# Second-layer weight chunks of 256 neighbouring rows, two to a partition, in a one-core mixture-of-experts encoder layer

## The chip, the cores and the metric

One core of a Trainium2 chip runs the whole layer. The metric is the device time of one execution in microseconds. The kernel before takes 1170.18 us, the median of 3 runs (1169.88 to 1171.66).

## What is computed

The layer takes 256 tokens of width 1024, all in float32. First comes the token mixer: RMSNorm, a combined projection, four heads of gated linear attention and eight heads of ordinary attention, and an output projection with a residual. Then comes the mixture of experts, in which most of the time lies:

```
logits = xt @ w_router + b_router              # 32 experts, each token goes to its best 4
gates  = softmax(top 4 logits)
per expert e, for the rows routed to it:
    h      = xb @ w1[e] + b1[e]                # 1024 -> 2048
    h_glu  = min(h[:, :1024], 7)
    h_lin  = clip(h[:, 1024:], -7, 7)
    act    = h_glu * sigmoid(1.702 * h_glu) * (h_lin + 1)      # the SwiGLU tile
    y      = act @ w2[e] + b2[e]               # 1024 -> 1024
out = h + sum over the 4 experts of gate * y, then a last RMSNorm
```

The weights of one expert are 8 MB of `w1[e]` and 4 MB of `w2[e]`, and those of all 32 experts are read from HBM once.

## The kernel before

**Stages.** The engines' programs are written out by hand, one after the other, and talk by semaphores. About the first 165 us are the token mixer, the router and its tables. Then `expert(n, q, it)` (L1303 to L1352 on TensorE, L931 to L950 on VectorE, L558 to L572 on ScalarE) runs once for each expert, in rounds of 64 tokens (`CAP`) per expert. The first four experts are written out, and the other 28 are a loop of bodies of four.

**Weights.** A ring of 16 slots, each 8 KB in every partition, holds chunks of weights. An expert has 12 chunks: 8 of the first layer (128 rows of `w1[e]`, each 8 KB, one to a partition, L316) and 4 of the second (L319). Each is one DMA of 1024 KB, all issued by SyncE in the order of use. SyncE waits at `refill` (L350 to L358) until TensorE has used the chunk that had the slot (`chunk_used`), and then issues the next one, 16 chunks ahead. Four more chunks lie in the scratch area `work` in the beginning (`load_early`).

**One expert on TensorE.** The hidden layer is kept as a tile of 128 partitions by 512 columns: partition `j * 64 + c` is token slot c with half j of the hidden columns (`GROUPS` is 2, `FG` is 512). (1) L1238 puts the bias into banks 2 and 5. (2) The first layer, L1319: 8 chunks of 4 matmuls each; between them four `combine` matmuls (L1288) add the expert before to the output. (3) `gather(n + 1)` (L1281): 48 short bf16 matmuls fetch the tokens of the next expert. (4) L1332: four transposes of `lin`, the SwiGLU tile, which VectorE has ready after L943, L944, L946 and L949. (5) L1341: two transposes of the gates. (6) ScalarE copies the four transposes out of bank 5 into `hidT` (L563). (7) The second layer, L1349: 4 chunks of 4 matmuls, with `hidT` as the stationary operand and the weights streaming. ScalarE copies the result out (L571), and VectorE's L943 of the next expert starts when its first layer is done.

**The rows of a second-layer chunk.** In the kernel before, chunk s holds, in partition p, rows `s * 128 + p` and `512 + s * 128 + p` of `w2[e]`: two separate runs of 4 KB (`by_half`, L278). Transposed block s of `lin` has the hidden columns `s * 128 + p` of both halves side by side, so that one block serves one chunk.

In the built program the operand that a transpose loads as its weights is `lin`, and the identity matrix streams.

Of the kernel before, what the change touches and what calls it, by code (L numbers as in the profile page):

```python
# [27 lines left out]
P = 128  # L28
SEQ = 256
TILES = SEQ // P  # L30
D = 1024
# [24 lines left out]
CAP = 64  # L56
GROUPS = P // CAP
ROUNDS = SEQ // CAP
FG = FF // GROUPS
SUB = FG // P  # L60
# [7 lines left out]
PEELED = EARLY_AT + EARLY + SLOTS  # L68
W1_CHUNKS = KD
W2_CHUNKS = SUB  # L70
PER_EXPERT = W1_CHUNKS + W2_CHUNKS
UNROLL = 4
PER_BODY = UNROLL * PER_EXPERT
assert PER_BODY % SLOTS == 0 and EXPERTS % UNROLL == 0 and GROUPS * 1024 == SLOT
LOADS_PER_BODY = PER_BODY // SLOTS
assert all(c % PER_EXPERT for c in range(EARLY_AT, EARLY_AT + EARLY))
TABLE = ROUNDS * EXPERTS + UNROLL
# [26 lines left out]
def encoder_layer(nc, x, w_in, w_out, w_router, w1, b1, w2, b2, gate_w, columns, rows, final_g,  # L104
                  c_keep, c_front, later, split, out):
    ctx = ExitStack()
    with ctx:
# [11 lines left out]
        ident, iota, before, ones = (ckeep[:, i * P:(i + 1) * P] for i in range(4))  # L119
# [104 lines left out]
        lin = back(FG)  # L224
        sig = back(FG)
        hidT = back(SUB, P)
# [12 lines left out]
        bank = [ctx.enter_context(nc.psum_tensor(f"bank{i}", [P, 512], F32))[:, :] for i in range(8)]  # L239
# [26 lines left out]
        def slot_of(c):  # L266

            return (c - EARLY) % SLOTS

        def first_slot_of(c):  # L270

            return c % SLOTS

        def slot(s):
            return ring[:, s * SLOT:(s + 1) * SLOT]

        def by_half(chunk):

            return chunk.rearrange("p (j n) -> p j n", n=D)


        @block.sync
        def _(sp):
# [16 lines left out]
            def load_b1(n, e):  # L300
                sp.dma_start(b1_sb[n % 2].rearrange("j (g f) -> j g f", g=2),
                             b1[e].rearrange("(g j f) -> j g f", g=2, j=GROUPS)).then_inc(b1_in[n % 2], 16)
# [10 lines left out]
            def load(to, loaded, e, r):  # L313

                if r < W1_CHUNKS:
                    sp.dma_start(to, w1[e, r * P:(r + 1) * P, :]).then_inc(loaded, 16)  # L316
                else:
                    s = r - W1_CHUNKS
                    sp.dma_start(by_half(to), w2[e].rearrange("(j s p) n -> s p j n", j=GROUPS, p=P)[s]).then_inc(loaded, 16)  # L319

            def first_ring(s):
                load(slot(s), slot_in[s], s // PER_EXPERT, s % PER_EXPERT)

            def load_early(i):
                load(early[i], early_in[i], (EARLY_AT + i) // PER_EXPERT, (EARLY_AT + i) % PER_EXPERT)

# [22 lines left out]
            def refill(it, used, e):  # L349

                c = SLOTS + used
                q, r = divmod(c, PER_EXPERT)
                if r == 0:
                    sp.wait_ge(S.chunk_used, it * PER_BODY + ((q - 2) * PER_EXPERT + W1_CHUNKS))
                    load_b1(q, e)
                sp.wait_ge(S.chunk_used, it * PER_BODY + (used + 1))
                load(slot(slot_of(c)), slot_in[slot_of(c)], e, r)
# [15 lines left out]
            start = PEELED - SLOTS  # L373
# [5 lines left out]
            last = rounds * bodies + whole  # L379
# [616 lines left out]
        def _(pe):  # L996
            mm = nc.tensor.matmul
# [4 lines left out]
            for pair in range(KD // 2):  # L1002
                if pair >= 2:
                    pe.wait_ge(S.xT_v if pair == 2 else S.xT_a, 2)
                for k in (2 * pair, 2 * pair + 1):
                    for t in range(TILES):
                        o = (k % 2) * SEQ + t * P
                        last = nc.tensor.transpose(bank[6 + pair % 2][:, o:o + P], h[:, t, k * P:(k + 1) * P], ident)
                last.then_inc(S.xT_ps, 1)

            def xT(k, t=None):
                return turned[:, k, :] if t is None else turned[:, k, t * P:(t + 1) * P]


            for k in range(KD):
# [4 lines left out]
                def put(o, l, r, first):  # L1020
                    return mm(o, l, r, start=a and first, stop=z, skip_group_check=True)  # L1021
# [6 lines left out]
                for t in range(TILES):  # L1028
                    put(bank[3 + t][:, :], xT(k, t), w[:, C_AQ:C_AK], True)
                    last = put(bank[5][:, t * SEQ:(t + 1) * SEQ], xT(k, t), w[:, C_AK:D_IN], t == 0)  # L1030
# [20 lines left out]
            for k in range(KD):  # L1051
                for t in range(TILES):
                    last = mm(bank[6 + t][:, :], xT(k, t), w_in_sb[:, k, C_GV:C_GR], start=k == 0, stop=k == KD - 1)
# [16 lines left out]
            for k in range(KD):  # L1070
                for t in range(TILES):
                    last = mm(bank[3 + t][:, :], xT(k, t), w_in_sb[:, k, C_GR:C_ZG], start=k == 0, stop=k == KD - 1)
# [129 lines left out]
            def router(t):  # L1202
                for k in range(KD):
                    if k % 4 == 0:
                        pe.wait_ge((S.hT_v, S.hT_a)[k // 4], t + 1)
                    last = mm(bank[6][:, t * EXPERTS:(t + 1) * EXPERTS], xT(k, t), wr_sb[:, k, :], start=k == 0, stop=k == KD - 1)
                return last
# [4 lines left out]
            for t in range(TILES):  # L1212
                if t == 1:
                    pe.wait_ge(S.ogla_sb, TILES)
                for k in range(4):
                    for nb in range(2):
                        last = mm(bank[Y[2 * t + nb]][:, :], xT(4 + k, t), w_out_att[:, k, nb * 512:(nb + 1) * 512],  # L1217
                                  start=k == 0, stop=False, skip_group_check=True)
# [4 lines left out]
            for t in range(TILES):  # L1223
                pe.wait_ge((S.glaT_v, S.glaT_a)[t], 1)
                for k in range(4):
                    if t == 1 and k == 2:
                        turn_h(0)
                    for nb in range(2):
                        last = mm(bank[Y[2 * t + nb]][:, :], xT(k, t), w_out_gla[:, k, nb * 512:(nb + 1) * 512],  # L1229
                                  start=False, stop=k == 3, skip_group_check=True)  # L1230
# [5 lines left out]
            def start_hidden(g, q):  # L1236

                mm(bank[(2, 5)[g]][:, :], split_of(q % 2), b1_sb[q % 2][:, g * FG:(g + 1) * FG], start=True, stop=False,  # L1238
                   skip_group_check=True)
# [7 lines left out]
            last = router(1)  # L1247
# [45 lines left out]
            def loaded(q, r, it):  # L1293

                c = q * PER_EXPERT + r
                first = isinstance(it, int)
                if first and c < EARLY_AT:
                    pe.wait_ge(slot_in[first_slot_of(c)], (c // SLOTS + 1) * 16)
                    return slot(first_slot_of(c))
                if first and c < EARLY_AT + EARLY:  # L1300
                    pe.wait_ge(early_in[c - EARLY_AT], 16)
                    return early[c - EARLY_AT]
                pe.wait_ge(slot_in[slot_of(c)], (it * LOADS_PER_BODY + ((c - EARLY) // SLOTS + 1)) * 16)  # L1303
                return slot(slot_of(c))

            def expert(n, q, it, first=False, second=False):


                if not first:
                    pe.wait_ge(b1_in[q % 2], (it * (UNROLL // 2) + (q // 2 + 1)) * 16)  # L1310
                    start_hidden(1, q)
                    pe.wait_ge(S.res_ready, n)
                    start_hidden(0, q)
                pe.wait_ge(S.xg_ready, n + 1)
                for k in range(W1_CHUNKS):
                    chunk = loaded(q, k, it)
                    for j in range(GROUPS):
                        for g in range(2):
                            last = mm(bank[(2, 5)[g]][j * CAP:(j + 1) * CAP, :], xg[:, k * CAP:(k + 1) * CAP],  # L1319
                                      chunk[:, g * FF + j * FG:g * FF + (j + 1) * FG], start=False, stop=k == KD - 1,  # L1320
                                      skip_group_check=True)
                    last.then_inc(S.chunk_used, 1)

                    if second and k % 2 == 0:
                        start_row(k // 2)
                    if not first and k % 2 == 1:
                        combine(k // 2)
                gather(n + 1)

                pe.wait_ge(S.hid_ready, n + 1)  # L1330
                for s in range(SUB):
                    last = nc.tensor.transpose(bank[5][:, s * P:(s + 1) * P], lin[:, s * P:(s + 1) * P], ident)  # L1332
                last.then_inc(S.hidT_ps, 1)

                pe.wait_ge(S.gated_ready, n + 1)
                if first:
                    pe.wait_ge(S.gateT_sb, 1)
                else:
                    pe.wait_ge(S.gatedT_sb, n)
                for t in range(TILES):  # L1340
                    last = nc.tensor.transpose(bank[7][:, t * P:(t + 1) * P], gated[:, t, :], ident)  # L1341
                last.then_inc(S.gatedT_ps, 1)
                pe.wait_ge(S.hidT_sb, n + 1)

                for s in range(W2_CHUNKS):
                    chunk = by_half(loaded(q, W1_CHUNKS + s, it))
                    for half in range(GROUPS):
                        for j in range(GROUPS):
                            last = mm(bank[2][j * CAP:(j + 1) * CAP, :], hidT[:, s, half * CAP:(half + 1) * CAP],  # L1349
                                      chunk[:, half, j * 512:(j + 1) * 512], start=s == 0 and half == 0,  # L1350
                                      stop=s == SUB - 1 and half == GROUPS - 1, skip_group_check=True)
                    last.then_inc(S.chunk_used, 1)  # L1352

            for t in range(TILES):
# [17 lines left out]
            for nb in range(2):  # L1372
                last = mm(bank[5 + nb][:, :], ones[FIN_G_ROW:FIN_G_ROW + 1, :], fin_g[:, nb * 512:(nb + 1) * 512],
                          start=True, stop=True)
# [48 lines left out]
```

## Time and profile before

| | |
|---|---|
| Median of 3 runs | 1170.18 us (1169.88 to 1171.66) |
| Span of the profiled execution | 1170.7 us |
| The profiled execution's own time outside its span | not given apart |
| TensorE matmul busy | 1113.7 us, 95% |
| VectorE, ScalarE, GpSimd busy | 212.8, 117.3, 18.9 us |
| DMA packets' time, share of 16 engines' span | 89.7% |
| Mean granted TensorE clock | 0.984 of full speed |

A matmul in float32 stands in the profile as two MATMUL records with a LDWEIGHTS record each. "PE" is TensorE's matmul side, "PEld" its weight loads, "SPq" SyncE's queue. "Idle before" is the time that an engine stood still before an instruction, with what released it. A busy TensorE says little by itself; what matters is which wait ends last in each stage.

### The profile page before, as it was taken

Reading aid. Unit: us, or ns where it says so; the run is one execution under the profiler, and the core shown is the slowest. Engines: PE = TensorE matmul, PEld = TensorE weight load, DVE = VectorE, ACT = ScalarE, POOL = GpSimd, SP = SyncE. Lnnn points to the kernel's source line nnn. Section 1 sums busy time; section 2 is a strip of 40 time slices with the busy share of each in tenths; the row PEclk is TensorE's granted clock in tenths of the full one; section 3 lists DMA queues with packets and bytes.
Section 4 is the critical chain, followed back from the end, with each engine's and each line's share of the span. In section 5 each row is a group of like instructions: output and inputs, shape, how many; then the busy total and the mean of one; then the engine's idle time right before and its main releaser. Section 6 shows DMA issues by size and latency. Waiting matters only on the chain.

```text
span 1170.7 us, 14556 instructions
## 1 busy us (share of the span) xinstructions
PE 1113.7 (95%) x5873; PEld 440.4 (38%) x5873; DVE 212.8 (18%) x491; ACT 117.3 (10%) x226; POOL 18.9 (2%) x18
## 2 busy tenths in 40 slices
PE   7997989999999999999999999999999999999996
PEld 4645443333333333333333333333333333333332
DVE  1186251111111110111111111111111111011113
ACT  1053120000000000000000000000000000000002
POOL 0010020000000000000000000000000000000000
PEclk9997979999999999999999999999999999999998
DMA  9655529988999999999999999999999999999940
GB/s 372 176 204 225 218 113 405 345 358 324 407 411 404 408 406 412 405 410 405 413 400 408 408 405 408 406 404 411 413 406 413 408 405 404 413 410 406 405 169 36
DMA packets 75952, 420.28 MB, mean 359 GB/s; under 512 B 6869, under 2 KB 7129, under 8 KB 42138
## 3 DMA queue, kind: packets, MB, share of 16 engines
q1 hardware_dynamic: 75930, 419.98, 89.7%
q8 instruction: 15, 0.25, 0.1%
q14 instruction: 7, 0.06, 0.0%
HBM read 418.91 MB, written 1.05 MB: 359 GB/s over the span
## 4 chain that ended last, share of the span: by engine, by line
PE 83%; DVE 10%; ACT 3%; issue 3%; DMA 0%; POOL 0%; SPq 0%; POOLq 0%; DVEq 0%
PE bank L1319 40%; PE bank L1349 20%; PE bank L1288 9%; PE bank L1238 5%; PE bank L1021 4%; DVE work L949 2%; DVE work L946 2%; DVE work L944 2%; PE bank L1332 2%; ACT work L563 2%; PE bank L1229 1%; PE bank L1217 1%; DMA h<-in_x_dram 0%; ACT work L513 0%; DVE work L943 0%
## 5 line engine op out<-in xcount | busy, mean ns | idle before, releaser
L1319 PE MATMUL bank<-ring,work 128*64 128x512 f32 x2016 | 468.0, 602 | 0.4 <-DVE work L928 0.4
L1319 PEld LDWEIGHTS bank<-ring,work 128*64 128x64 f32 x2016 | 154.2, 136 | 298.2 <-issue 297.3
L1349 PE MATMUL bank<-ring,work 128*64 128x512 f32 x1024 | 228.5, 599 | 15.5 <-ACT work L563 15.5
L943 DVE TENSOR_SCALAR work<-bank 128x512 f32<-128x512 f32 x32 | 22.1, 692 | 829.0 <-PE bank L1319 829.0
L1288 PE MATMUL bank<-work 64*128 64x512 f32 x256 | 141.2, 640 | 0.7 <-ACT work L571 0.7
L1349 PEld LDWEIGHTS bank<-ring,work 128*64 128x64 f32 x1024 | 71.7, 137 | 151.7 <-issue 134.0
L560 ACT ACTIVATE work<-work 128x512 f32<-128x512 f32 x32 | 20.2, 630 | 639.2 <-DVE work L943 639.2
L1288 PEld LDWEIGHTS bank<-work 64*128 64x128 f32 x256 | 37.2, 184 | 102.7 <-issue 101.1
L1238 PE MATMUL bank<-biases,split_sb 2*128 2x512 f32 x128 | 64.5, 622 | 0.0
L1281 PE MATMUL bank<-work,tok 128*128 128x64 bf16 x1056 | 50.8, 194 | 0.0
L1281 PE MATMUL bank<-work 128*128 128x64 bf16 x528 | 48.9, 195 | 1.2 <-DVE work L921 1.2
L1281 PEld LDWEIGHTS bank<-work,tok 128*128 128x128 bf16 x1056 | 47.4, 99 | 0.0
L1281 PEld LDWEIGHTS bank<-work 128*128 128x128 bf16 x528 | 33.5, 99 | 25.6 <-issue 25.6
L571 ACT ACTIVATE work<-bank 128x512 f32<-128x512 f32 x32 | 19.1, 597 | 223.4 <-PE bank L1349 223.4
L1238 PEld LDWEIGHTS bank<-biases,split_sb 2*128 2x128 f32 x128 | 21.2, 185 | 40.7 <-issue 25.3
L1332 PE MATMUL bank<-ckeep,work 128*128 128x128 f32 x128 | 21.0, 286 | 9.9 <-DVE work L949 9.9
L397 POOL TENSOR_TENSOR stat<-stat 128x1 f32<-128x1 f32 (+2 forms) x8 | 9.1, 1136 | 1105.2 <-DVE stat L604 1105.2
L563 ACT ACTIVATE work<-bank 128x512 f32<-128x512 f32 x32 | 19.1, 597 | 68.3 <-PE bank L1332 68.3
L928 DVE TENSOR_TENSOR work<-bank,col 128x512 f32<-128x512 f32 x33 | 22.6, 684 | 0.8 <-PE bank L1281 0.8
L949 DVE TENSOR_TENSOR work<-work 128x512 f32<-128x512 f32 x32 | 22.1, 692 | 1.1
L946 DVE SCALAR_TENSOR_TENSOR work<-work 128x512 f32<-128x512 f32 x32 | 22.1, 692 | 1.1
L936 DVE TENSOR_SCALAR work<-ckeep,work 128x128 f32<-128x128 f32 x64 | 19.3, 344 | 15.4 <-PE bank L1341 15.4
(185 smaller groups left out, 479.2 us busy)
## 6 DMA issues: line engine op xcount, KB each, us to landing
ring<-in_w_dram SPq DMA_DIRECT2D x380, 1024.0 KB, 7.9
ring<-in_w_in_dram SPq DMA_DIRECT2D x8, 1168.0 KB, 15.9
work<-in_w_dram SPq DMA_DIRECT2D x4, 1024.0 KB, 8.2
ring<-in_w_out_dram SPq DMA_DIRECT2D x2, 1024.0 KB, 27.5
ring<-in_w_out_dram SPq DMA_DIRECT2D x1, 2048.0 KB, 29.7
h<-in_x_dram SPq DMA_DIRECT2D x2, 512.0 KB, 4.5
out_dram<-tok SPq DMA_DIRECT2D x4, 256.0 KB, 2.2
biases<-in_b_dram SPq DMA_DIRECT2D x32, 8.0 KB
```

What stands on the lines that cost most here:

```text
L563: nc.scalar.activation(hidT, bank[5][:, :].rearrange("p (s q) -> p s q", q=P), ACT.Copy)\
L928: nc.vector.tensor_tensor(xg.rearrange("p (k c) -> p k c", c=CAP), bank[6][:, :].rearrange("p (k c) -> p k c", c=CAP), ffn_g.rearrange("p ...
L944: nc.vector.tensor_scalar(lin, bank[5][:, :], LIMIT, -LIMIT, ALU.min, ALU.max).then_inc(S.dve_step, 1)
L946: nc.vector.scalar_tensor_tensor(lin, lin, 1.0, glu, ALU.add, ALU.mult).then_inc(S.dve_step, 1)
L949: nc.vector.tensor_tensor(lin, lin, sig, ALU.mult).then_inc(S.hid_ready, 1)
L1021: return mm(o, l, r, start=a and first, stop=z, skip_group_check=True)
L1238: mm(bank[(2, 5)[g]][:, :], split_of(q % 2), b1_sb[q % 2][:, g * FG:(g + 1) * FG], start=True, stop=False, skip_group_check=True)
L1281: last = mm(bank[6][:, k * CAP:(k + 1) * CAP], parts[t][i][:, k * P:(k + 1) * P], onehot[:, t, :], start=i == 0 and t == 0, stop=i == PART ...
L1288: last = mm(bank[Y[i]][:, :], gatedT[j * CAP:(j + 1) * CAP, t, :], res[j * CAP:(j + 1) * CAP, :], start=False, stop=stop, skip_group_check ...
L1319: last = mm(bank[(2, 5)[g]][j * CAP:(j + 1) * CAP, :], xg[:, k * CAP:(k + 1) * CAP], chunk[:, g * FF + j * FG:g * FF + (j + 1) * FG], star ...
L1332: last = nc.tensor.transpose(bank[5][:, s * P:(s + 1) * P], lin[:, s * P:(s + 1) * P], ident)
L1349: last = mm(bank[2][j * CAP:(j + 1) * CAP, :], hidT[:, s, half * CAP:(half + 1) * CAP], chunk[:, half, j * 512:(j + 1) * 512], start=s == ...
```

## The change

Second-layer chunk s now holds rows `s * 256` to `s * 256 + 255` of `w2[e]`, and partition p the rows `s * 256 + 2p` and `s * 256 + 2p + 1`, one run of 8 KB. Chunks 0 and 1 belong to half 0 of the hidden columns, chunks 2 and 3 to half 1. For the stationary operand to fit, a transposed block takes every second column of `lin`: block `b * 2 + r` has the columns `b * 256 + 2p + r`. Each transpose's weight load therefore reads 128 float32 values that lie 8 bytes apart, not 4. The number, sizes and order of all instructions on each engine are as before, and so is every wait.

```diff
+PAIR = 2
+BLOCKS = FG // (PAIR * P)
...
                 else:
                     s = r - W1_CHUNKS
-                    sp.dma_start(by_half(to), w2[e].rearrange("(j s p) n -> s p j n", j=GROUPS, p=P)[s]).then_inc(loaded, 16)
+                    sp.dma_start(to, w2[e].rearrange("(s p j) n -> s p (j n)", j=PAIR, p=P)[s]).then_inc(loaded, 16)
...
                 pe.wait_ge(S.hid_ready, n + 1)
-                for s in range(SUB):
-                    last = nc.tensor.transpose(bank[5][:, s * P:(s + 1) * P], lin[:, s * P:(s + 1) * P], ident)
+                pairs = lin.rearrange("p (b c r) -> p b c r", c=P, r=PAIR)
+                for b in range(BLOCKS):
+                    for r in range(PAIR):
+                        s = b * PAIR + r
+                        last = nc.tensor.transpose(bank[5][:, s * P:(s + 1) * P], pairs[:, b, :, r], ident)
                 last.then_inc(S.hidT_ps, 1)
...
                 for s in range(W2_CHUNKS):
-                    chunk = by_half(loaded(q, W1_CHUNKS + s, it))
-                    for half in range(GROUPS):
+                    chunk = by_row(loaded(q, W1_CHUNKS + s, it))
+                    half, b = divmod(s, BLOCKS)
+                    for r in range(PAIR):
                         for j in range(GROUPS):
-                            last = mm(bank[2][j * CAP:(j + 1) * CAP, :], hidT[:, s, half * CAP:(half + 1) * CAP],
-                                      chunk[:, half, j * 512:(j + 1) * 512], start=s == 0 and half == 0,
-                                      stop=s == SUB - 1 and half == GROUPS - 1, skip_group_check=True)
+                            last = mm(bank[2][j * CAP:(j + 1) * CAP, :], hidT[:, b * PAIR + r, half * CAP:(half + 1) * CAP],
+                                      chunk[:, r, j * 512:(j + 1) * 512], start=s == 0 and r == 0,
+                                      stop=s == SUB - 1 and r == PAIR - 1, skip_group_check=True)
                     last.then_inc(S.chunk_used, 1)
```

## Rows read from the trace of the kernel before

**Rows 1.** The page's totals: busy us (share) xinstructions, and the DMA queue with packets.

```profile
PE 1113.7 (95%) x5873; PEld 440.4 (38%) x5873; DVE 212.8 (18%) x491; ACT 117.3 (10%) x226; POOL 18.9 (2%) x18
...
DMA packets 75952, 420.28 MB, mean 359 GB/s; under 512 B 6869, under 2 KB 7129, under 8 KB 42138
...
q1 hardware_dynamic: 75930, 419.98, 89.7%
```

**Rows 2.** All waits of TensorE that the profile names: us in total, times, longest us.

```profile
PE bank L1349 <- ACT work L563: 15.5, 32, 0.5
PE bank L1332 <- DVE work L949: 9.9, 32, 1.3
PE bank L1008 <- DMA h<-in_x_dram: 7.6, 1, 7.6
```

**Rows 3.** SyncE's waits: us in total, times, longest us.

```profile
SPq L316 <- PE bank L1349: 245.4, 118, 5.4
SPq L316 <- PE bank L1319: 233.0, 116, 3.5
SPq L319 <- PE bank L1319: 227.8, 124, 10.5
```

**Rows 4.** Windows, each from L943 to the next L943; last columns: granted clock, DMA share, GB/s.

```profile
183.32:220.57 37.25, 35.45 (x169) 11.50 (x169) 4.20 (x9) 2.10 (x4) 0.00 (x0) 0.95 1.00 393
251.44:282.30 30.86, 30.12 (x163) 11.02 (x163) 4.20 (x9) 2.10 (x4) 0.00 (x0) 1.00 0.86 345
405.85:436.71 30.86, 30.12 (x163) 11.04 (x163) 4.20 (x9) 2.10 (x4) 0.00 (x0) 1.00 1.01 407
1116.25:1147.12 30.87, 30.13 (x163) 11.03 (x164) 4.20 (x10) 2.10 (x4) 0.00 (x0) 1.00 0.27 106
```

**Rows 5.** The chain of waits from 407.1 us: start us, us, what.

```profile
407.17 0.70 DVE work L946
...
407.89 0.70 DVE work L949
...
408.64 0.67 PE bank L1332 x4
...
409.33 0.60 ACT work L563
...
409.99 1.07 PE bank L1349 x3
```

**Rows 6.** Timeline of the same place: start us, us, what [idle before <-releaser].

```profile
408.64 0.42 PEld L1332 LDWEIGHTS bank<-ckeep,work 128*128 128x128 f32 x4 [0.40 <-DVE work L949]
408.64 0.65 PE L1332 MATMUL bank<-ckeep,work 128*128 128x128 f32 x4 [0.28 <-DVE work L949]
```

**Rows 7.** L1332's weight loads, ns min/median/max; then page groups, busy us, mean ns.

```profile
L1332 PEld LDWEIGHTS bank<-ckeep,work x128: 137/141/143, 186.1 to 1150.2; 128*128 128x128 f32 x128
...
L1319 PEld LDWEIGHTS bank<-ring,work 128*64 128x64 f32 x2016 | 154.2, 136 | 298.2 <-issue 297.3
...
L1288 PEld LDWEIGHTS bank<-work 64*128 64x128 f32 x256 | 37.2, 184 | 102.7 <-issue 101.1
...
L1281 PE MATMUL bank<-work,tok 128*128 128x64 bf16 x1056 | 50.8, 194 | 0.0
```

**Rows 8.** Windows inside one expert; last columns as in rows 4.

```profile
419.00:423.00 4.00, 4.00 (x17) 1.43 (x18) 0.00 (x0) 0.00 (x0) 0.00 (x0) 1.00 1.01 426
...
409.00:413.00 4.00, 3.53 (x19) 1.34 (x19) 1.12 (x5) 0.87 (x2) 0.00 (x0) 1.00 1.02 410
```

**Rows 9.** Timeline: when SyncE issues, around the same expert.

```profile
401.37 4.98 SPq L319 DMA_DIRECT2D ring<-in_w_dram  x3
...
412.10 15.70 SPq L316 DMA_DIRECT2D ring<-in_w_dram  x8
```

**Rows 10.** The page's median time from issue to landing of the ring's chunks, in us.

```profile
ring<-in_w_dram SPq DMA_DIRECT2D x380, 1024.0 KB, 7.9
```

**Rows 11.** A window in the first expert's second layer; last columns as in rows 4.

```profile
187.60:191.00 3.40, 3.40 (x10) 0.97 (x11) 0.36 (x3) 0.09 (x1) 0.00 (x0) 0.50 1.03 413
```

More of the change, by code:

```diff
@@ L275, in slot, with by_row @@
             return ring[:, s * SLOT:(s + 1) * SLOT]
-        def by_half(chunk):
-            return chunk.rearrange("p (j n) -> p j n", n=D)
+        def by_row(chunk):
+            return chunk.rearrange("p (r n) -> p r n", n=D)
         @block.sync
```

## The prediction

> **What bounds the kernel now.** I read the page's totals first, then TensorE's and SyncE's waits, then windows one expert long, and last the chain of waits inside one expert.
>
> The totals leave two candidates: TensorE is busy for 95% of the span, and the DMA engines for 89.7% [rows 1]. Neither share says which one the other waits for. The waits do. TensorE waits for a DMA once, 7.6 us at the very start for `x`, and never for a chunk of weights; in the experts its named waits are for VectorE before the transposes and for ScalarE before the second layer, 32 times each, 9.9 and 15.5 us in all [rows 2]. SyncE waits for TensorE to give chunks free, 245.4 + 233.0 + 227.8 = 706 us [rows 3]. The transfers follow TensorE, and not the other way round.
>
> The windows say it more strongly. From one L943 to the next an expert takes 30.86 us when the DMA engines are busy for a share of 0.86, 30.86 us at 1.01, and 30.87 us at 0.27, near the end, when hardly a chunk is left to fetch [rows 4]. TensorE is busy for 30.12 or 30.13 us of each. So in the experts the time is TensorE's 30.1 us plus 0.74 us of idle time, and neither the transfers' speed nor their traffic shows in it. The 32 L943 lie in 183.32 to 1147.12 us: 31 periods, of which the first is 37.25 us and the others nearly alike.
>
> The 0.74 us of idle time lies at the activation. The chain ends on VectorE with L946 and L949 (L943 and L944 stand before them), then come the four transposes L1332 (0.67 us), ScalarE's copy L563 (0.60 us), and the second layer L1349 [rows 5]. TensorE has nothing else to do between L949 and L1349 but the six transposes. So whatever is added to L1332 is added to the expert, 32 times.
>
> **The change part by part.**
>
> *The transfers of the second layer.* 128 of the 384 chunks are fetched in runs of 8 KB and no longer of 4 KB. 32 experts x 4 chunks x 256 runs = 32,768 of the 42,138 packets under 8 KB [rows 1] become 16,384 of 8 KB. What is that worth to the DMA engines? SyncE issues L319's chunks from 401.37 us and L316's from 412.10 us [rows 9], and a chunk lands a median 7.9 us after its issue [rows 10]; so the window 409 to 413 us carries second-layer chunks, and 419 to 423 us first-layer chunks, whose runs are already 8 KB. They show 410 and 426 GB/s at the same full share [rows 8]. Four chunks, 4.19 MB, would take 9.8 us at 426 GB/s and not 10.2 us: 0.4 us of DMA time less per expert. All of it lies beside TensorE's work, and I count it as 0. Its cover is TensorE's period: an expert needs 12.58 MB, or 8.39 / 426 + 4.19 / 410 = 19.7 + 10.2 = 29.9 us, against 30.86. If that cover were gone, the 0.4 us would count in full (rival 2). The change only makes the cover thicker, to 29.5.
>
> *Order and use of the chunks.* SyncE issues as many DMAs at the same points with the same waits. A chunk holds the same 8 KB per partition at the same place in its slot, and the four matmuls on it stream the same halves of 512 columns with 64 stationary columns each. Only which block of `hidT` goes with which chunk differs, and all four blocks come from one copy, L563, before the first of these matmuls. This costs 0 and moves no wait: the release of each chunk still stands after its fourth matmul.
>
> *The four transposes.* Their streaming side, the identity, is as before; so are their writes to bank 5 and the copy behind them. What changes is the weight load, which now reads every second float32 of `lin`. The trace of before has no strided weight load, so I bound it. Below, the cost is 0: reading 128 values spread over twice the bytes gives no reason to be quicker than reading them side by side. Above, each load of 141 ns [rows 7] takes twice as long with nothing of it hidden: 4 x 0.141 x 32 = 18.0 us. Between the ends, the rows say what hides a load. The four loads together are busy for 0.42 us and the four multiplications follow them at that pace, 0.105 us each, although one load lasts 141 ns: a load runs under the multiplication before it [rows 6, 7]. Only the first has none before it, because TensorE has been idle for 0.28 us. What reading more costs there: a load of 128 columns is 184 ns and one of 64 is 136 ns [rows 7], 48 ns for 64 columns. If a step of two makes 128 columns cost like 192 to 256, that is 0.048 to 0.096 us on the first load, and times 32, 1.5 to 3.1 us. I take 0, because of the gather's loads, the nearest row on how fast TensorE can read weights: 33 gathers of 48 matmuls, each with a load of 128 bf16 columns, or 256 bytes per partition, are busy for 50.8 us [rows 7], 0.032 us each or 8.0 bytes per ns. A transpose's load has 0.105 us. Its 512 bytes need 4.9 bytes per ns in that time; if the gaps count as if they were read, 1024 bytes need 9.8. The former lies well within what the gather shows, the latter a fifth above it, which is why rival 1 stays alive.
>
> A rule bears on this. The Trainium skill, "Advanced Engine Details and Errata", section SBUF Cachelines, says that SBUF has lines of 16 bytes, that at least two hits on a line are needed for full speed, and that a different line for each access costs. A step of two float32 gives exactly two hits per line, so by that rule the loads cost nothing more, on the edge of it; a step of four would pay. No row of this trace tests it.
>
> *Sum.* 0 + 0 + 0 against a profiled span of 1170.7 us, whose time outside the span isn't given; the span is 0.5 us above the median and within the spread of the 3 runs. I set the forecast against the median: **1170.2 us**.
>
> **The rivals.** What a measurement of this kernel can tell from no change is about 0.2%, 2.3 us.
>
> 1. *The strided loads become the pace of the transposes (slower).* If a load's read takes longer than the 0.105 us of the multiplication that covers it, all four are exposed. At twice the pace L1332 takes 0.42 us more in each expert, and L563 and L1349 start that much later: 0.42 x 32 = 13.4 us, 1183.6 us. For it: nothing lies between L949 and L563 but these transposes [rows 5]. Against it: if only the wanted bytes count, the gather's loads read faster than this asks for [rows 7]. It decides from 0.105 us of reading on. Its mild form, only the first load longer, gives 1.5 to 3.1 us: 1171.7 to 1173.3.
>
> 2. *The transfers bound the experts after all (faster).* Their share is 1.01 for most of the run [rows 4], and 29.9 us of transfers is only 1.0 us below the period. If they set the period, 0.4 us comes off in each of the some 27 experts at that share: 10.8 us, 1159.4 us. Against it: no wait for a chunk in [rows 2], and the same period at a share of 0.27 [rows 4]. I see almost no room for it. The Trainium skill's page "Perfetto Trace Analysis", section What "DMA-bound" means, says that large descriptors are what matters where the DMA engines bind; by it this change would pay here if the share alone were looked at.
>
> 3. *The granted clock shifts.* In the first expert's second layer TensorE runs at 0.50 (the lower level, 1.2 GHz) for 3.40 us, right behind the idle time at its activation [rows 11]. At 2.4 GHz the same work takes 1.7 us, so losing this stretch gives 1168.5 us, and one more like it 1171.9. This stays within 0.2%.
>
> 4. *The change doesn't do what it says*: the DMA still goes out in 4 KB packets. Time as before, 1170.2 us, since the transfers are hidden either way.
>
> **How the numbers follow.** No change, rivals 3 and 4 with it: 0.83, at 1170.2. Rival 1 in full: 0.08. Its mild form: 0.05, of which 0.03 stays within 0.2%. Rival 2: 0.04. So faster 0.04, same 0.83 + 0.03 = 0.86, slower 0.08 + 0.02 = 0.10. The range goes from the clock's 1168.5 to the mild form's upper end, 1173.3, and leaves out rival 2 and the full rival 1, 0.12 together.
>
> **What would show it.** Right: from L943 to the next L943 again 30.87 us; the transposes' loads at about 141 ns, and four transposes in 0.67 us; packets under 8 KB down from 42,138 to about 9,400; the window of second-layer chunks at some 426 GB/s; SyncE's waits for TensorE longer, since chunks land sooner; TensorE still with no wait for a chunk. Rival 1: the four transposes longer than 0.67 us, with L563 idle that much longer. Rival 2: a period under 30.8 us. The prediction is wrong if the transposes take over 0.07 us more per expert, or if the time before the first L943, 183.32 us, moves by over 2 us, which nothing here leads me to expect.

## The result and the profile after

The changed kernel takes 1173.41 us (median of 6 runs, 1172.38 to 1174.94), the kernel before 1170.69 us in the same comparison (6 runs, 1168.87 to 1171.66). The ratio is 1.0029 with a 95% interval of 1.0017 to 1.0040: slower by 0.3%, 2.7 us. The forecast was 1170.2 us and no change; the measured time lies just above the top of the range, 1173.3. The six times of each kernel fall in two groups of three, 1172.4 and 1174.4 to 1174.9 us for the changed kernel, 1168.9 to 1170.2 and 1171.2 to 1171.7 us for the kernel before, and each median lies between its groups.

The page's totals of the changed kernel answer to [rows 1]:

```profile
PE 1116.2 (95%) x5873; PEld 442.9 (38%) x5873; DVE 212.7 (18%) x491; ACT 117.3 (10%) x226; POOL 18.9 (2%) x18
...
DMA packets 59568, 420.28 MB, mean 358 GB/s; under 512 B 6869, under 2 KB 7129, under 8 KB 9370
...
q1 hardware_dynamic: 59546, 419.98, 88.9%
```

The 8 KB runs are there: packets under 8 KB fell from 42,138 to 9,370, and the DMA engines' share from 89.7% to 88.9%. TensorE's busy time grew by 2.5 us with the same number of instructions. Its waits are those of [rows 2], to the tenth in the experts:

```profile
PE bank L1355 <- ACT work L565: 15.5, 32, 0.5
PE bank L1337 <- DVE work L951: 9.9, 32, 1.3
PE bank L1010 <- DMA h<-in_x_dram: 7.5, 1, 7.5
```

So no wait of TensorE was added and none taken away; something that TensorE or the chain behind it does takes longer. Two windows of the changed kernel, with the columns of [rows 4]. The first is one expert, from L945 (the old L943) to the next L945; the second carries second-layer chunks and answers to the last of [rows 8]:

```profile
405.89:436.85 30.96, 30.22 (x163) 11.12 (x163) 4.20 (x9) 2.10 (x4) 0.00 (x0) 1.00 1.00 412
408.00:412.00 4.00, 3.26 (x31) 1.76 (x29) 2.16 (x6) 0.87 (x2) 0.00 (x0) 1.00 1.02 426
```

An expert takes 30.96 us instead of 30.86, and TensorE is busy for 30.22 us of it instead of 30.12. The transfers got faster, 426 GB/s instead of 410. That is one window of 4 us; the same window in the 12 experts behind it shows 420 to 424 GB/s, and 410 or 411 in the kernel before. So the gain is some 3%, and it is worth nothing. The experts behind the first all show the difference. The last L945 of the changed kernel comes 929.23 us after its second one; in the kernel before the same 30 periods take 1147.12 - 220.57 = 926.55 us [rows 4]. That is 2.68 us over 30 experts, 0.089 us each:

```profile
220.07 0.69 DVE L945 TENSOR_SCALAR work<-bank 128x512 f32<-128x512 f32 x1 [32.60 <-PE bank L1321]
...
1149.30 0.69 DVE L945 TENSOR_SCALAR work<-bank 128x512 f32<-128x512 f32 x1 [26.10 <-PE bank L1321]
```

The place of the loss shows in the chain of waits of the changed kernel, which answers to [rows 5]:

```profile
407.22 0.70 DVE work L948
...
407.94 0.70 DVE work L951
...
408.69 0.76 PE bank L1337 x4
...
409.48 0.61 ACT work L565
...
410.12 1.07 PE bank L1355 x3
```

The four transposes take 0.76 us and not 0.67; all other links have their old length to 0.01 us. The durations of these instructions in the changed kernel and in the kernel before (ns min/median/max, first and last start) say how:

```profile
L1337 PEld LDWEIGHTS bank<-ckeep,work x128: 194/209/222, 185.5 to 1152.4; 128*128 128x128 f32 x128
L1337 PE MATMUL bank<-ckeep,work x128: 281/283/387, 185.5 to 1152.6; 128*128 128x128 f32 x128
```

```profile
L1332 PE MATMUL bank<-ckeep,work x128: 272/273/330, 186.1 to 1150.3; 128*128 128x128 f32 x128
```

A load takes 209 ns instead of 141 [rows 7]. Of the four multiplications, three went from 273 to 283 ns. The maximum, which belongs to the first of a group, whose load nothing covers, went from 330 to 387. 57 + 3 x 10 = 87 ns per expert, and times 32 that is 2.8 us. The records overlap, so durations alone could mislead, but the start times say the same. As medians over the 32 experts, the four multiplications start 2, 167, 277 and 386 ns after the first load in the kernel before, and 2, 224, 344 and 464 ns after it in the changed one: 57 ns later behind the first, then some 10 ns more for each.

### The profile page after: what moved, and what is told of

Same layout as the page of the kernel before. It is cut to its first block, busy times and chain, and to the rows that moved or that the text cites. A ratio compares the mean times of both kernels' runs of the same rounds, so it can differ in the third digit from the quotient of the medians.

```text
span 1173.0 us, 14556 instructions
## 1 busy us (share of the span) xinstructions
PE 1116.2 (95%) x5873; PEld 442.9 (38%) x5873; DVE 212.7 (18%) x491; ACT 117.3 (10%) x226; POOL 18.9 (2%) x18
## 2 busy tenths in 40 slices
DMA packets 59568, 420.28 MB, mean 358 GB/s; under 512 B 6869, under 2 KB 7129, under 8 KB 9370
## 3 DMA queue, kind: packets, MB, share of 16 engines
q1 hardware_dynamic: 59546, 419.98, 88.9%
## 4 chain that ended last, share of the span: by engine, by line
PE 83%; DVE 10%; ACT 3%; issue 2%; DMA 0%; POOL 0%; SPq 0%; POOLq 0%; DVEq 0%
PE bank L1321 40%; PE bank L1355 19%; PE bank L1290 9%; PE bank L1240 5%; PE bank L1023 3%; PE bank L1337 2%; DVE work L951 2%; DVE work L948 2%; DVE work L946 2%; ACT work L565 2%; PE bank L1231 1%; PE bank L1219 1%; ACT work L515 0%; DMA h<-in_x_dram 0%; DVE work L945 0%
## 5 line engine op out<-in xcount | busy, mean ns | idle before, releaser
L1355 PE MATMUL bank<-ring,work 128*64 128x512 f32 x1024 | 228.5, 599 | 15.5 <-ACT work L565 15.5
L945 DVE TENSOR_SCALAR work<-bank 128x512 f32<-128x512 f32 x32 | 22.1, 692 | 829.0 <-PE bank L1321 829.0
L1337 PE MATMUL bank<-ckeep,work 128*128 128x128 f32 x128 | 23.8, 309 | 9.9 <-DVE work L951 9.9
L1337 PEld LDWEIGHTS bank<-ckeep,work 128*128 128x128 f32 x128 | 17.8, 208 | 13.7 <-DVE work L951 13.7
## 6 DMA issues: line engine op xcount, KB each, us to landing
ring<-in_w_in_dram SPq DMA_DIRECT2D x8, 1168.0 KB, 15.5
```

The costliest lines, as they stand in the source:

```text
L1337: last = nc.tensor.transpose(bank[5][:, s * P:(s + 1) * P], pairs[:, b, :, r], ident)
L1355: last = mm(bank[2][j * CAP:(j + 1) * CAP, :], hidT[:, b * PAIR + r, half * CAP:(half + 1) * CAP], chunk[:, r, j * 512:(j + 1) * 512], sta ...
```

## The experiments

Theory A: the weight loads with a step of two columns are the whole cost. Theory B: the 8 KB transfers disturb TensorE. Theory C: the difference comes from outside the experts. All comparisons below have the kernel before on the same chip. The first four experiments share its 26 runs (median 1170.04 us), the last four its 7 runs (1170.62 us).

**e1_runs_only.** The changed kernel with the transposes of before:

```diff
-                        last = nc.tensor.transpose(bank[5][:, s * P:(s + 1) * P], pairs[:, b, :, r], ident)
+                    last = nc.tensor.transpose(bank[5][:, s * P:(s + 1) * P], lin[:, s * P:(s + 1) * P], ident)
```

> Only the 8 KB runs are kept; the transposes read neighbouring columns again, so that a chunk's rows of w2 meet other hidden columns than they belong to (same work, other pairing). Theory A (the weight load with a step of two columns is the whole cost): four transposes back at 0.67 us, loads at 141 ns, period of an expert 30.87 us, time level with before (ratio 1.000, within 0.001). Theory B (the 8 KB transfers disturb TensorE or what feeds it): period near 30.96 us, ratio near 1.0025. Theory C (the measured 2.7 us comes from outside the experts): period 30.87 us and ratio still near 1.0025.

Measured: 1169.87 us (12 runs), ratio 0.9998 (0.9988 to 1.0007). One expert lies between these two rows of its timeline, 30.87 us:

```profile
403.10 0.69 DVE L945 TENSOR_SCALAR work<-bank 128x512 f32<-128x512 f32 x1 [26.09 <-PE bank L1321]
433.97 0.69 DVE L945 TENSOR_SCALAR work<-bank 128x512 f32<-128x512 f32 x1 [26.06 <-PE bank L1321]
```

The loads are back at 140 ns. Theories B and C fall: with the 8 KB runs alone, the time is that of before. The 30 periods behind the first expert take 926.55 us (217.82 to 1144.37), as in the kernel before to the hundredth.

**e2_step_only.** The kernel before with the changed kernel's transposes and its own 4 KB runs:

```diff
-                    last = nc.tensor.transpose(bank[5][:, s * P:(s + 1) * P], lin[:, s * P:(s + 1) * P], ident)
+                        last = nc.tensor.transpose(bank[5][:, s * P:(s + 1) * P], pairs[:, b, :, r], ident)
```

> Only the transposes' step of two columns is put into the kernel before; the chunks are fetched in 4 KB runs as before, so the pairing of rows and hidden columns is off (same work). Theory A: loads near 209 ns, period near 30.96 us, 32 x 0.09 = 2.9 us, ratio 1.0025. Theory B: period 30.87 us, ratio 1.000. Theory C: period 30.87 us.

Measured: 1174.37 us (6 runs), ratio 1.0033 (1.0021 to 1.0044). The transposes of this kernel, and one expert of 30.96 us:

```profile
L1337 PEld LDWEIGHTS bank<-ckeep,work x128: 194/209/222, 184.2 to 1149.5; 128*128 128x128 f32 x128
L1337 PE MATMUL bank<-ckeep,work x128: 281/283/387, 184.2 to 1149.6; 128*128 128x128 f32 x128
```

```profile
402.90 0.69 DVE L945 TENSOR_SCALAR work<-bank 128x512 f32<-128x512 f32 x1 [26.10 <-PE bank L1321]
433.86 0.69 DVE L945 TENSOR_SCALAR work<-bank 128x512 f32<-128x512 f32 x1 [26.06 <-PE bank L1321]
```

The same durations as in the changed kernel, with the old transfers, and 929.24 us for the 30 periods (217.08 to 1146.32) against the changed kernel's 929.23. The step of two alone makes the whole difference, and theory A stands: one half of the change costs 2.8 us and the other is worth 0.

**e5_step4.** As e2_step_only, but the values of a load lie 16 bytes apart, and the pairing is off here too:

```diff
-PAIR = 2
+PAIR = 4
```

> As the kernel before, but the transposes step by four columns (16 bytes), so the pairing of rows and hidden columns is off. If a load's cost grows with the bytes it spans (+68 ns from step one to two), loads near 345 ns, the multiplications paced by them at some 0.25 us, period 31.4 to 31.6 us, 17 to 22 us more in all. If each value then needs a line of its own and two were free, the same or worse. If any step but one costs the same: loads 209 ns, period 30.96 us, 2.9 us more.

Measured: 1173.39 us (6 runs), ratio 1.0030 (1.0019 to 1.0042).

```profile
L1337 PEld LDWEIGHTS bank<-ckeep,work x128: 195/212/222, 184.7 to 1150.0; 128*128 128x128 f32 x128
L1337 PE MATMUL bank<-ckeep,work x128: 283/285/388, 184.7 to 1150.1; 128*128 128x128 f32 x128
```

The cost does not grow with the bytes spanned: a step of four is 212 ns, a step of two 209, a step of one 141. Of the two steps tried, both pay about 70 ns. My expectation of 345 ns was wrong, and the third case written down, that any step but one costs the same, held for these two steps. The prediction drew on a rule here: by the Trainium skill, "Advanced Engine Details and Errata", section SBUF Cachelines, at least two hits on a line of 16 bytes are needed for full speed. The prediction took two hits to be enough. The trace does not bear that out for this weight load: a step of two gives two hits and pays 68 ns, and a step of four, with one hit, pays only 3 ns more. The measurement decides.

**e3_sorted.** The 8 KB runs kept, the sorting moved from TensorE's weight load to VectorE's last multiplication, and the transposes reading its new tile:

```diff
-                nc.vector.tensor_tensor(lin, lin, sig, ALU.mult).then_inc(S.hid_ready, 1)
+                by_parity = [a.rearrange("p (b c r) -> p b r c", c=P, r=PAIR) for a in (lin, sig)]
+                nc.vector.tensor_tensor(glu.rearrange("p (b r c) -> p b r c", c=P, r=PAIR), *by_parity, ALU.mult)\
+                    .then_inc(S.hid_ready, 1)
```

> The change with the sorting moved to VectorE: its last multiplication of the SwiGLU tile reads both operands with a step of two columns and writes the result side by side into another tile, and the transposes read neighbouring columns. Theory A: loads at 141 ns, period 30.87 us if VectorE reads with a step of two at its old 692 ns, ratio 1.000; if that multiplication gets longer by x ns, the period gets longer by x as well, since it stands right ahead of the transposes. Theory B: period 30.96 us or more.

Measured: 1169.93 us (11 runs), ratio 1.0001 (0.9993 to 1.0010). The multiplication and the transposes' loads of this kernel:

```profile
L952 DVE TENSOR_TENSOR work<-work x32: 691/692/693, 184.6 to 1146.6; 128x512 f32<-128x512 f32 x32
```

```profile
L1336 PEld LDWEIGHTS bank<-ckeep,work x128: 138/140/143, 185.3 to 1147.7; 128*128 128x128 f32 x128
```

VectorE reads both operands with a step of two at its old 692 ns. This version does all that the change does, at no cost, and still gains nothing: the transfers are hidden.

**e8_covered.** Does a strided load cost where a long multiplication covers it? The kernel before, with `hidT` interleaved:

```diff
-        hidT = back(SUB, P)
+        hidT = back(SUB * P)
+        mixed = hidT.rearrange("p (q s) -> p s q", s=SUB)
...
-                nc.scalar.activation(hidT, bank[5][:, :].rearrange("p (s q) -> p s q", q=P), ACT.Copy)\
+                nc.scalar.activation(mixed, bank[5][:, :].rearrange("p (s q) -> p s q", q=P), ACT.Copy)\
...
-                            last = mm(bank[2][j * CAP:(j + 1) * CAP, :], hidT[:, s, half * CAP:(half + 1) * CAP],
+                            last = mm(bank[2][j * CAP:(j + 1) * CAP, :], mixed[:, s, half * CAP:(half + 1) * CAP],
```

> The kernel before with hidT kept interleaved, so that the weight loads of the second layer read with a step of four float32 (ScalarE writes hidT with that step). If a strided load costs only where nothing covers it: loads near 200 ns and not 137, the second layer's matmuls still one pair per 427 ns, only the first load of each expert exposed, 0.05 to 0.06 us each, 1.6 to 1.9 us in all, ratio 1.0015, plus whatever ScalarE's copy gets longer. If a strided load costs on each load, as with the transposes' 0.011 us behind the first: 32 x 0.011 = 0.35 us per expert, 11 us, ratio 1.0096.

Measured: 1186.68 us (4 runs), ratio 1.0140 (1.0123 to 1.0157). The loads and matmuls of its second layer, then ScalarE's copy (from the groups of the costliest instructions: busy us, mean ns):

```profile
L1350 PEld LDWEIGHTS bank<-ring,work x1024: 192/193/218, 186.1 to 1171.0; 128*64 128x64 f32 x171
L1350 PE MATMUL bank<-ring,work x1024: 592/592/707, 186.1 to 1171.4; 128*64 128x512 f32 x171
```

```profile
L564 ACT ACTIVATE work<-bank 128x512 f32<-128x512 f32 x32 | 34.4, 1075 | 68.2 <-PE bank L1333 68.2
```

The median of the 1024 loads is 193 ns and no longer 137, and that of the matmuls stays at 592 ns. The group's busy time is 228.8 us. The 228.5 us of the kernel before are no fair measure for it, because they hold a stretch at the lower clock [rows 11] that this run doesn't have; e3_sorted, without such a stretch and with neighbouring columns, shows:

```profile
L1354 PE MATMUL bank<-ring,work 128*64 128x512 f32 x1024 | 226.8, 595 | 15.5 <-ACT work L565 15.5
```

The 2.0 us more are 0.06 us per expert, the one exposed load. Behind it the pace is the same: from the second pair of records of an expert's second layer to the last the median is 6.02 us in e3_sorted and here. Covered by 0.43 us of multiplication, the strided load costs nothing. What this kernel loses lies elsewhere. Its expert takes 31.41 us between these two rows, 0.54 more than before:

```profile
406.04 0.69 DVE L944 TENSOR_SCALAR work<-bank 128x512 f32<-128x512 f32 x1 [26.64 <-PE bank L1320]
437.45 0.69 DVE L944 TENSOR_SCALAR work<-bank 128x512 f32<-128x512 f32 x1 [26.60 <-PE bank L1320]
```

ScalarE's copy, which now writes with a step of four, went from 597 to 1075 ns, and that is 0.48 us of the 0.54. The other 0.06 is what one exposed load got longer, 56 ns by the medians. Of the two cases written down, the covered one held; the copy I had left open.

**e6_split_copy.** If the 0.7 us between L949 and L1349 is where something is to be had, the copy in it is the larger link. The kernel before, with the copy cut in two:

```diff
-                nc.scalar.activation(hidT, bank[5][:, :].rearrange("p (s q) -> p s q", q=P), ACT.Copy)\
-                    .then_inc(S.hidT_sb, 1)
+                for part in range(2):
+                    nc.scalar.activation(hidT[:, 2 * part:2 * part + 2, :],
+                                         bank[5][:, part * 256:(part + 1) * 256].rearrange("p (s q) -> p s q", q=P), ACT.Copy)\
+                        .then_inc(S.hidT_sb, 1)
...
-                pe.wait_ge(S.hidT_sb, n + 1)
...
                 for s in range(W2_CHUNKS):
+                    if s % 2 == 0:
+                        pe.wait_ge(S.hidT_sb, 2 * n + (s // 2 + 1))
```

> The kernel before with ScalarE's copy of the four transposes cut into two copies of two blocks, and the second layer waiting for the first of them alone. If the wait from the transposes to the second layer is what an expert's 0.74 us of idle time consists of, the second layer starts as much earlier as a copy of 256 columns (378 ns) is shorter than one of 512 (597 ns): 0.22 us per expert, 7.0 us in all, ratio 0.994. Rival: the idle time is taken by something else (the gate transposes, the second half of the copy), and the ratio is 1.000.

Measured: 1163.21 us (4 runs), ratio 0.9936 (0.9920 to 0.9953). That is 7.4 us less, where 7.0 were expected, and the rival falls. TensorE's wait for ScalarE fell from 15.5 to 8.7 us:

```profile
PE bank L1351 <- ACT work L564: 8.7, 32, 0.3
```

**e7_two_banks.** As before it, and blocks 2 and 3 go to bank 7, so that ScalarE may read bank 5 while TensorE goes on:

```diff
-                    last = nc.tensor.transpose(bank[5][:, s * P:(s + 1) * P], lin[:, s * P:(s + 1) * P], ident)
-                last.then_inc(S.hidT_ps, 1)
+                    if s == 2:
+                        last.then_inc(S.hidT_ps, 1)
+                        if not first:
+                            pe.wait_ge(S.gatedT_sb, n)
+                    last = nc.tensor.transpose(bank[(5, 7)[s // 2]][:, s * P:(s + 1) * P], lin[:, s * P:(s + 1) * P], ident)
```

> As e6_split_copy, but blocks 2 and 3 are transposed into bank 7, so that ScalarE can copy blocks 0 and 1 as soon as they are there. 0.22 us more per expert, 0.44 us in all, period 30.44 us, 14 us less, ratio 0.988. Rival: TensorE itself is busy until then with transposes and the gain stays near e6's 7 us.

Measured: 1156.11 us (4 runs), ratio 0.9876 (0.9860 to 0.9893). The chain of waits of this kernel at an activation; L1338 is the four transposes, L1344 the two of the gates, L1352 the second layer:

```profile
402.48 0.70 DVE work L951
...
403.23 0.66 PE bank L1338 x4
403.89 0.22 PE bank L1344 x2
404.10 0.04 issue
404.14 6.22 PE bank L1352 x27
```

ScalarE is gone from the chain, and the second layer follows the transposes with a gap of 0.04 us. The expected 14 us came. This is the fastest version here, by 14.5 us against the kernel before in the same comparison. It differs from e6_split_copy in two things, the second bank and the signal after two transposes and not four; the earlier signal with all four blocks in bank 5 was not tried, so which of the two is needed is not shown.

**e9_both.** With an expert at 30.44 us, the cover over the 4 KB runs is down to some 0.5 us. Do the 8 KB runs pay now? This is e7_two_banks with the 8 KB runs and the sorting of e3_sorted:

```diff
-                    sp.dma_start(by_half(to), w2[e].rearrange("(j s p) n -> s p j n", j=GROUPS, p=P)[s]).then_inc(loaded, 16)
+                    sp.dma_start(to, w2[e].rearrange("(s p j) n -> s p (j n)", j=PAIR, p=P)[s]).then_inc(loaded, 16)
...
-                nc.vector.tensor_tensor(lin, lin, sig, ALU.mult).then_inc(S.hid_ready, 1)
+                by_parity = [a.rearrange("p (b c r) -> p b r c", c=P, r=PAIR) for a in (lin, sig)]
+                nc.vector.tensor_tensor(glu.rearrange("p (b r c) -> p b r c", c=P, r=PAIR), *by_parity, ALU.mult)\
+                    .then_inc(S.hid_ready, 1)
```

> e7_two_banks with the 8 KB runs, the sorting done by VectorE's last multiplication. With an expert near 30.44 us and 29.9 us of transfers at 4 KB runs, the cover is 0.5 us. If the transfers stay hidden, the same time as e7_two_banks within 0.1%. If they begin to show there, this kernel is faster than e7_two_banks by up to 0.4 us per expert, 11 us.

Measured: 1156.92 us (4 runs), ratio 0.9880 (0.9863 to 0.9896). One expert of e7_two_banks and one of this kernel, columns as in [rows 4]:

```profile
400.43:430.87 30.44, 30.13 (x163) 11.04 (x164) 4.20 (x10) 2.27 (x5) 0.00 (x0) 1.00 1.02 415
```

```profile
400.19:430.63 30.44, 30.13 (x163) 11.03 (x164) 4.21 (x10) 2.27 (x5) 0.00 (x0) 1.00 1.01 416
```

The same period to 0.01 us, so the first case written down held. Even here TensorE sets it, at 30.13 us of busy time, and the longer runs are worth nothing.

## Why the prediction was wrong, point by point

- **What bounds the kernel: right.** TensorE's own work and the chain at the activation set an expert's time. e1_runs_only and e9_both show that faster transfers change nothing, although the DMA engines' share is 1.0. Rival 2 falls.
- **The transfers' gain of 0.4 us per expert, hidden: right in kind, a little large.** Both rates came from one window of 4 us each. At the 420 to 426 GB/s measured, four chunks take 9.8 to 10.0 us and not 10.2, so the gain is 0.2 to 0.4 us. It is hidden: the ratio is 0.9998 with the runs alone. Rival 4 falls with the packets under 8 KB, down to 9,370. SyncE's three waits for TensorE are 715 us in all and were 706 [rows 3]:

```profile
SPq L318 <- PE bank L1355: 249.9, 118, 5.5
SPq L318 <- PE bank L1321: 232.9, 116, 3.4
SPq L321 <- PE bank L1321: 232.2, 124, 10.6
```

- **The order of the chunks at 0: right.** All waits of TensorE in the experts are as before.
- **The four transposes at 0: the step that failed.** The term "I take 0, because of the gather's loads" measured 2.8 us, 0.09 us per expert, over the 0.07 that the prediction itself named as the sign of being wrong. The gather's figure itself is sound, though the row given for it holds only 1056 of the 1584 loads: in the timeline, one gather's 48 multiplications take 1.57 us, 0.033 us each. The use made of it is what failed. The gather's loads show how fast TensorE takes in one load after another with neighbouring columns; they say nothing of what a step does to one load. I divided bytes by time and compared the quotients, and e5_step4 shows that bytes spanned are not what counts. The nearer estimate stood in the sentence before it: an exposed first load costs 0.048 to 0.096 us, 1.5 to 3.1 us in all. The first load measured 57 ns. What that estimate missed is that the three covered transposes also got 10 ns longer each, at a cover of only 0.105 us.
- **Rival 1 in full (13.4 us): not so.** The loads did not become the pace at twice its length; the 0.105 us from one transpose to the next would have become 0.21; by the start times it went from 0.109 to 0.120. Its mild form, to which I gave 0.05, is the larger part of what happened (57 of 87 ns). The place on the chain and the exposed first load were written down and priced, and the forecast went against them: with no row that shows the operation, 0.05 was far too little. That the time fell outside the range at all is partly chance: 1170.2 + 2.8 = 1173.0 would lie within it, but in this comparison the kernel before came out at 1170.69, and the changed kernel 2.7 us above that.
- **Rival 3, the granted clock: it was there, and did not decide.** A stretch at 0.50 behind the first expert's activation stands in the profiled runs of the kernel before [rows 11] and of the changed one. In e1_runs_only and e2_step_only (and in the other profiled runs) it is absent, and the first period is 1.7 us shorter: 35.55 and 35.64 us in these two windows, e1_runs_only first, where [rows 4] have 37.25.

```profile
182.27:217.82 35.55, 33.75 (x169) 11.07 (x169) 4.20 (x10) 2.10 (x4) 0.00 (x0) 1.00 1.01 419
```

```profile
181.44:217.08 35.64, 33.84 (x169) 11.17 (x169) 4.20 (x10) 2.10 (x4) 0.00 (x0) 1.00 1.02 417
```

So the profiled span of e2_step_only is 1170.0 us although its experts are as slow as the changed kernel's, whose span is 1173.0: 1.7 of these 3.0 us lie in the first period, and 1.3 before the first L945, which comes at 181.44 and at 182.75 us. Whether the clock also makes the two groups in the times above is not shown, since one run of each kernel was profiled. One span can't tell 2.8 us here; the period of an expert, which repeats, tells 0.09 us.

## What to carry to other kernels

Ask of each re-laid-out load who pays for the new order, and whether he stands on the chain: here the gain went to the DMA engines, whose transfers stayed hidden even with an expert at 30.44 us, and the cost to the one chain on which TensorE waits. A strided weight load is free under a long multiplication and costs where it is the first after idle time or its cover is short; let an engine sort that reads with a step at no cost, as VectorE did here. And look at the idle gap itself before the transfers: cutting one copy in two and spreading four transposes over two PSUM banks took 14.5 us off.

## What was not expected of the hardware

- A float32 weight load of TensorE takes some 70 ns longer with a step of two columns (141 to 209 ns at 128 columns), and no more with a step of four (212 ns). At 64 columns a step of four adds 56 ns (137 to 193). Why these two steps cost, and nearly the same, stays open; steps of three and above four were not tried.
- ScalarE's copy from PSUM to SBUF of 128 x 512 float32 takes 1075 ns and not 597 when it writes with a step of four. VectorE's multiplication of the same size, reading two operands with a step of two, keeps its 692 ns. A write with a step was not tried on VectorE, nor a read with one on ScalarE.
- With the share of the DMA engines at 1.0, an expert takes as long as with 0.27 [rows 4], and shortening it to 30.44 us only raised the rate to 415 GB/s. A full share was no sign of a bound.
